# Folding the norm factors out of TensorE's input between two transformer blocks: weighted parts first, means later

## Chip, cores and metric

The kernel runs on one core of one Trainium2 chip. The metric is the device time of one execution in microseconds (us), as the median of several runs.

## The reference, cut to what matters

One sequence of 256 tokens of width 1024 runs through two layers of a first block and then through two layers of a second block. The change sits where the first block ends and the second block's first layer (its NSA attention) begins:

```python
# end of each layer of the first block
x = x + y @ w_out[i]
gate = sigmoid(rms_norm(x, ple_norm_g[i]) @ ple_w_gate[i])
x = x + gate * (p[i] @ ple_w_proj[i])
# end of the first block, start of the second
x = rms_norm(x, final_norm_g)
h = rms_norm_2(x, attn_norm[0])
proj = h @ a_w_in[0]          # queries, k/v of three branches, gates, q_mem
kc, vc = compress_blocks(k_cmp, ...), compress_blocks(v_cmp, ...)   # blocks @ w1, gelu, @ w2
kv = rms_norm_2(mem, mem_norm[l]) @ w_mem_kv[l]    # memory, l = 0 and 1
```

An RMS norm multiplies each token by one number (the reciprocal root of the mean of its squares) and each column by a weight.

## The kernel before, in words

**Data.** Activations stand transposed, 128 features on the partitions and 256 tokens along the free axis, in eight chunks (`X`). All large products run in split fp32: each operand is a rounded high part plus a low part, and a product is three matmuls (high by high, high by low, low by high). A weight piece is an item of up to 1024 columns: it comes from HBM into `raw` (three tiles of two items each, loaded by SP's queue; a tile is loaded again only when VectorE has made the low parts of the tile three back), ScalarE copies it to its high part (`split_hi`, L369) and VectorE subtracts to get the low part (`split_lo`, L382). The split pieces stand in a ring of slots. The first stages have NW = 3 slots. From the event named in `MORE_AT` on there are six, as the top of the arena is free then; `items_until` (L344) sets how far ScalarE and VectorE split ahead of the item that a stage asks for: two pieces with three slots, five with six. A piece can be split into a slot only when TensorE has used the piece that was there. Each engine has its order written out by hand, in program order of `layer_*`, `out_*`, `between_*`, `nsa_*`; `q.wait_ge(*got(event))` waits for another engine.

**PSUM** has seven banks that go round (`begin_bank`, L395): a product that begins waits until the bank's last user, seven banks back, has been read out. The eighth (`mean_bank`) holds the means.

**Out stage** (`out_pe`, `out_v`, `out_a`, `out_g`, for both layers of the first block): four pairs of chunks of `w_out` (16 matmul triples each), with X updated after each; then four rounds of a gate pair (`ple_w_gate`, two items) and a projection pair (`ple_w_proj`, two items of 256 columns). In each round VectorE scales the gate (L1780), ScalarE takes the sigmoid (L1852), VectorE multiplies with the projection (L1784) and adds to X (L1787). In layer 1 ScalarE also squares the memory (L1841), TensorE takes its mean ("mem mean"), and after the last round VectorE makes 16 scaled chunks (`scaled_v`, L535), ScalarE the high parts (L498), VectorE and GpSimd the low parts (L502) of the memory for both layers of the second block.

**Between stage** (`between_*`): mean of X's squares, ln and exp on ScalarE (L508, L510), three Newton steps on VectorE (L514 to L518), X scaled (L1920), squared (L1932), summed on GpSimd (L476); meanwhile TensorE does the memory products of layer 0, "mem k" (two items) and "mem v" (two items).

**NSA stage** (`nsa_*`): second mean, the same chain again, 8 scaled chunks and their parts `HN`, with the memory products of layer 1 beside them; then row products `nrows` 0 and 1 (four items each), column products `zc` 0, 2 and 4 (two items each), `nrows` 2, the eight items of the compressed branch (L2296 to L2300), its transposes (L2307), the turned queries and keys, gelu, and the second compressed product (L2319). Then the attention in rounds, in which the softmax of the compressed branch (`cmp_pe_`, `cmp_v_`) is woven at hand-written places (`chain`).

Each stage starts on ScalarE, VectorE and GpSimd with a `barrier` that waits until all other engines have ended the stage before.

## Time and profile before

| | |
|---|---|
| median of 3 runs | 1318.05 us (1317.97 to 1319.31) |
| the profiled execution, whole | 1316.94 us |
| its span, first to last instruction | 1314.9 us |
| mean granted TensorE clock | 0.927 of full |
| TensorE matmul busy | 1139.5 us, 87% |
| VectorE busy | 951.3 us, 72% |
| ScalarE busy | 691.4 us, 53% |
| GpSimd busy | 153.4 us, 12% |
| HBM read | 164.9 MB, 126 GB/s over the span |

A time in the profile is in us from the first instruction. A group of instructions is named by its line in the kernel, its engine, and what it writes and reads; "idle before, releaser" is how long its engine stood still before it and who ended the wait. ps is PSUM, WH and WL are the ring's high and low parts, FR is a rounded part in the arena.

### The profile page before, as it was taken

Reading aid. Unit: us, or ns where it says so; the run is one execution under the profiler, and the core shown is the slowest. Engines: PE = TensorE matmul, PEld = TensorE weight load, DVE = VectorE, ACT = ScalarE, POOL = GpSimd, SP = SyncE. Lnnn points to the kernel's source line nnn. Section 1 sums busy time; section 2 is a strip of 40 time slices with the busy share of each in tenths; the row PEclk is TensorE's granted clock in tenths of the full one; section 3 lists DMA queues with packets and bytes.
Section 4 is the critical chain, followed back from the end, with each engine's and each line's share of the span. In section 5 each row is a group of like instructions: output and inputs, shape, how many; then the busy total and the mean of one; then the engine's idle time right before and its main releaser. Section 6 shows DMA issues by size and latency. Waiting matters only on the chain.

```text
span 1314.9 us, 24945 instructions
## 1 busy us (share of the span) xinstructions
PE 1139.5 (87%) x10437; PEld 1060.7 (81%) x10437; DVE 951.3 (72%) x1681; ACT 691.4 (53%) x1263; POOL 153.4 (12%) x113
## 2 busy tenths in 40 slices
PE   6699866979799858948976789999999979999997
PEld 6688865979678747848965579999999959999997
DVE  5787964666778855677677956888876655788873
ACT  5633246555532266555454755555665474555562
POOL 2000000110000001143000001223200001132220
PEclk9999986989899977988985989999999989999999
DMA  8332110444231103324531034554563703454461
GB/s 334 123 110 98 66 65 1 137 152 159 91 129 66 66 1 126 132 95 144 197 117 65 1 101 160 176 173 161 194 231 121 256 1 127 145 179 161 162 221 50
DMA packets 24735, 167.54 MB, mean 127 GB/s; under 512 B 2736, under 2 KB 2864, under 8 KB 8496
## 3 DMA queue, kind: packets, MB, share of 16 engines
q1 hardware_dynamic: 24624, 165.96, 36.1%
q8 instruction: 82, 1.34, 0.4%
q14 instruction: 29, 0.24, 0.1%
HBM read 164.90 MB, written 1.05 MB: 126 GB/s over the span
## 4 chain that ended last, share of the span: by engine, by line
PE 49%; DVE 28%; ACT 17%; issue 3%; DMA 2%; POOL 0%; DVEq 0%; SPq 0%; ACTq 0%; POOLq 0%
PE ps L428 10%; PE ps L425 9%; PE ps L423 9%; DVE WL L382 8%; ACT WH L369 4%; DVE FR L382 3%; PE ps L446 3%; PE ps L454 3%; PE ps L448 3%; PE ps L651 2%; ACT ARENA L756 2%; DMA raw<-wst_in 2%; ACT FR L369 1%; ACT L485 1%; ACT ARENA L2147 1%
## 5 line engine op out<-in xcount | busy, mean ns | idle before, releaser
L382 DVE TENSOR_TENSOR WL<-raw,WH 128x1024 fp32r<-128x1024 f32 (+4 forms) x225 | 273.4, 1238 | 103.8 <-ACT WH L369 103.5
L423 PE MATMUL ps<-FR,WH 128*128 128x256 f32 x1248 | 306.7, 286 | 20.0 <-ACT WH L369 16.6
L425 PE MATMUL ps<-FR,WH 128*128 128x256 f32 x1248 | 302.6, 283 | 1.4 <-DVE FR L494 1.0
L369 ACT ACTIVATE WH<-raw 128x1024 fp32r<-128x1024 f32 (+4 forms) x225 | 218.2, 988 | 102.2 <-PE ps L428 52.3
L423 PEld LDWEIGHTS ps<-FR,WH 128*128 128x128 f32 x1248 | 241.5, 193 | 25.2 <-ACT WH L369 13.7
L425 PEld LDWEIGHTS ps<-FR,WH 128*128 128x128 f32 x1248 | 241.2, 193 | 3.5 <-DVE FR L494 2.0
L423 PE MATMUL ps<-FR,FR 128*128 128x256 f32 x680 | 167.5, 284 | 2.9 <-ACT FR L369 2.3
L428 PE MATMUL ps<-FR,WL 128*128 128x256 f32 x1248 | 169.4, 278 | 0.3 <-DVE WL L382 0.3
L425 PE MATMUL ps<-FR,FR 128*128 128x256 f32 x680 | 166.4, 283 | 0.2 <-DVE FR L494 0.2
L428 PEld LDWEIGHTS ps<-FR,WL 128*128 128x128 f32 x1248 | 155.0, 189 | 0.6 <-DVE WL L382 0.6
L382 DVE TENSOR_TENSOR FR<-raw,FR 128x1024 fp32r<-128x1024 f32 (+2 forms) x100 | 126.7, 1292 | 28.8 <-ACT FR L369 28.7
L423 PEld LDWEIGHTS ps<-FR,FR 128*128 128x128 f32 x680 | 129.3, 190 | 4.8 <-ACT FR L369 3.7
L425 PEld LDWEIGHTS ps<-FR,FR 128*128 128x128 f32 x680 | 129.3, 190 | 0.6 <-DVE FR L494 0.4
L369 ACT ACTIVATE FR<-raw 128x1024 fp32r<-128x1024 f32 (+2 forms) x100 | 99.8, 1012 | 22.1 <-DMA raw<-wst_in 10.5
L2147 ACT ACTIVATE ARENA<-ARENA,vec 128x256 f32<-128x256 f32 x88 | 48.2, 595 | 113.2 <-DVE ARENA L2098 113.2
L2192 POOL TENSOR_TENSOR ARENA<-ARENA 128x256 f32<-128x256 f32 x44 | 78.5, 1785 | 217.4 <-ACT ARENA L2159 217.4
L476 POOL TENSOR_TENSOR ARENA<-ARENA 128x512 f32<-128x512 f32 x32 | 45.4, 1419 | 453.6 <-DVE FR L494 141.4
L428 PE MATMUL ps<-FR,FR 128*128 128x256 f32 x680 | 95.4, 282 | 0.0
L446 PE MATMUL ps<-WH,FR 128*128 128x512 f32 (+4 forms) x200 | 79.4, 401 | 16.3 <-DVE ZR L1509 8.4
L428 PEld LDWEIGHTS ps<-FR,FR 128*128 128x128 f32 x680 | 87.3, 190 | 0.0
L2106 DVE SCALAR_TENSOR_TENSOR ARENA<-ARENA,vec 128x254 f32<-128x254 f32 (+1 forms) x176 | 76.7, 476 | 1.6
L448 PE MATMUL ps<-WH,FR 128*128 128x512 f32 (+4 forms) x200 | 76.2, 385 | 0.0
(324 smaller groups left out, 1771.1 us busy)
## 6 DMA issues: line engine op xcount, KB each, us to landing
raw<-wst_in SPq DMA_DIRECT2D x124, 1024.0 KB, 5.0
raw<-wst_in SPq DMA_DIRECT2D x14, 768.0 KB, 4.3
raw<-wst_in SPq DMA_DIRECT2D x11, 896.0 KB, 4.8
raw<-wst_in SPq DMA_DIRECT2D x4, 968.0 KB, 4.7
raw<-wst_in SPq DMA_DIRECT2D x2, 912.0 KB, 4.6
cst<-cst_in SPq DMA_DIRECT2D x1, 1681.0 KB, 15.2
X<-xT_in SPq DMA_DIRECT2D x2, 512.0 KB, 6.3
ARENA<-memT_in SPq DMA_DIRECT2D x1, 1024.0 KB, 4.8
```

The source lines that it names most:

```text
L369: a.activation(hi[:, 0:cols], src, ACT.Copy).then_inc(*put("split_hi", ("hi", i)))
L382: v.tensor_tensor(lo[:, 0:cols], src, hi[:, 0:cols].bitcast(F32), SUB).then_inc(*put("split_lo", ("lo", i)))
L423: pe.matmul(out, hv[:, k, :], src.hi[:, c, :], start=k0 == 0 and k == ks[0], stop=False)
L425: pe.matmul(out, hv[:, k, :], src.lo[:, c, :], start=False, stop=False)
L428: ins = pe.matmul(out, lv[:, k, :], src.hi[:, k0 + k, :], start=False, stop=k0 + n == kc and k == ks[-1])
L446: pe.matmul(outs[b], src.hi[:, c, t], hv[:, k, :], start=c == 0, stop=False)
L448: pe.matmul(outs[b], src.lo[:, c, t], hv[:, k, :], start=False, stop=False)
L454: ins = pe.matmul(outs[b], src.hi[:, c, t], lv[:, k, :], start=False, stop=c == KC - 1)
L476: g_.tensor_tensor(sq[0], sq[0], sq[n], ADD).then_inc(*put("square_sum", ("summed", tag, 2 * n)))
L2106: v.scalar_tensor_tensor(u, p2[:, 256 * w:256 * w + 256 - d], vcol("conv_w_2", l, 44 * (2 - d) + c), u, MUL, ADD) \
L2147: a.activation(m.ub[2 * (i % 3) + w], m.pb[i % 3][:, 256 * w:256 * w + 256], ACT.Identity, bias=vcol("conv_b_2", l, c), scale=vcol("conv_w ...
L2192: g_.tensor_tensor(m.fb[n % 3], u[0], u[1], MUL).then_inc(*put("ffn_g", ("f", l, n)))
```

## The change

1. The ring has six slots from the last gate product of layer 1 on, before from "mem v" of layer 1 on. So the whole out stage of layer 1 splits five pieces ahead; the three upper slots wait for the end of layer 1.
2. `ple_w_proj` comes as one item of 1024 columns for two rounds (both layers), before as four items of 256 columns.
3. The memory's parts are made from the raw memory times its weight, without the norm's factor, in rounds 0 and 1 of the out stage of layer 1 (ScalarE high, VectorE low, GpSimd nothing). The factor is applied when the product is read out: to k along the tokens, to v as one number per partition, for which TensorE turns the factor (`columns_pe`). The factor's ln and exp move from round 2 to after the barrier that follows the out stage, and its Newton steps with them.
4. `HN` is made in the same way from X before the final norm, times the product of both norms' weights, in the four rounds. The two norms' factors are multiplied (`rs12`) and applied at the read-out of `zc` and `nrows`.
5. TensorE's order: mem k 0, mem v 0, turn, mem k 1, first mean, mem v 1, zc 0, zc 2, second mean and turn (`scale_pe`), nrows 0 and 1, compressed first half, nrows 2, compressed second half, zc 4, its transposes, turned queries. The `U` blocks and the rope follow on VectorE.
6. In the attention rounds the second compressed product, its rope and the softmax of the compressed branch are spread over five rounds, before over three.

Cut to its core (the moved buffers and the same edits on the other engines' orders are left out):

```diff
-MORE_AT = ("mem v", 1)
+MORE_AT = ("gate", 1, 4)
...
         if i < m:
             return w_slots[i % NW], i - NW
         j = i - m
+        if j < NW:
+            return w_slots[j], max(x for x in range(m - NW, m) if x % NW == j)
         return w_slots[j % (NW + NMORE)], (m - 1 if j < NW + NMORE else i - NW - NMORE)
...
-        ahead = ahead or (2 if n < first_more() else 4 if event[0] == "cmp1" else NW + NMORE - 1)
+        ahead = ahead or (2 if n <= first_more() else 4 if event[0] == "cmp1" else NW + NMORE - 1)
...
-            if i == first_more():
+            if i == first_more() + NW:
                 for e in ("PE", "V", "G"):
-                    q.wait_ge(*got("end", "T", e))
+                    q.wait_ge(*got("end", ("L", 1), e))
...
+        if c0 % 4 == 0:
+            proj_item[0] = take(("ple_w_proj", l, tuple(r(128 * c0, 128 * c0 + 512)), 0, 2), 1024)
+        i, hi, lo = proj_item[0]
+        hv, lv = (x.rearrange("p (k m) -> p k m", k=2) for x in (hi, lo))
+        src, tag = p_parts[l], ("p", l)
+        qpe.wait_ge(*got("hi", i))
+        qpe.wait_ge(*got("lo", i))
+        for x in range(2):
+            o, m = ps[:, 256 * x:256 * x + 256], slice(128 * (c0 % 4 + x), 128 * (c0 % 4 + x) + 128)
+            for k in range(2):
+                qpe.wait_ge(*got("hi", tag, k))
+                pe.matmul(o, hv[:, k, m], src.hi[:, k, :], start=k == 0, stop=False)
+                qpe.wait_ge(*got("lo", tag, k))
+                pe.matmul(o, hv[:, k, m], src.lo[:, k, :], start=False, stop=False)
+                ins = pe.matmul(o, lv[:, k, m], src.hi[:, k, :], start=False, stop=k == 1)
+        ins.then_inc(*put("item_used", ("w_proj", l, c0), *([("used", i)] if c0 % 4 else [])))
+        B.at_items["w_proj", l, c0] = len(B.plan)
...
-            for i in range(2):
-                feat("ple_w_proj", l, r(128 * (c0 + i), 128 * (c0 + i) + 128), p_parts[l], ("p", l), ps[:, 256 * i:256 * i + 256],
-                     "w_proj", l, c0, kc=2)
+            proj_pe(l, c0, ps)
...
+        if l == 1 and c0 < 4:
+            for i in range(2):
+                for c in r(2 * c0, 2 * c0 + 4):
+                    part_x_lo(v, q, mem_parts[i], ("mem", i), c, vcol("mem_norm_2", i, 0, 8), M)
...
-            elif c0 == 4:
-                ps, free = psum("mem mean")
-                q.wait_ge(*got("mem y"))
-                newton(v, q, "mem_v", mem_rs, ps[:, 0:S], 1e-6, mem_hs[0], ("mem rs",), free)
-                q.wait_ge(*own("mem_v"))
-            elif c0 == 6:
-                for i in range(2):
-                    if i:
-                        q.wait_ge(*got("lo", ("mem", 0), 6))
-                        q.wait_ge(*got("lo", ("mem", 0), 7))
-                    scaled_v(v, q, M, vcol("mem_norm_2", i, 0, 8), mem_parts[i], ("mem", i), mem_hs, bank=mem_rs)
+            else:
+                if c0 == 0:
+                    v.tensor_tensor(g12, vcol("final_norm_g", None, 0, 8), vcol("attn_norm_2", 0, 0, 8), MUL).then_inc(*put("ple_v", ("g12",)))
+                q.wait_ge(*own("ple_v"))
+                for c in (c0, c0 + 1):
+                    part_x_lo(v, q, HN, "HN", c, g12)
...
-            if l == 1 and c0 == 4:
-                q.wait_ge(*got("mem mean"))
-                table(a, LNEXP)
-                ps, _ = psum("mem mean")
-                a.activation(mem_hs[0], ps[:, 0:S], ACT.Ln, bias=C("eps6")).then_inc(*put("mem_a"))
-                q.wait_ge(*own("mem_a"))
-                a.activation(mem_hs[0], mem_hs[0], ACT.Exp, scale=-0.5).then_inc(*put("mem_a", ("mem y",)))
+            if l == 1 and c0 < 4:
+                for i in range(2):
+                    for c in r(2 * c0, 2 * c0 + 4):
+                        part_x_hi(a, mem_parts[i], ("mem", i), c, vcol("mem_norm_2", i, 0, 8), M)
...
-            elif c0 < 4:
-                pass
-        if l == 1:
-            q.wait_ge(*got("mem mean"))
-            for c0 in range(0, 8, 2):
+            else:
+                q.wait_ge(*got("g12"))
+                for c in (c0, c0 + 1):
+                    part_x_hi(a, HN, "HN", c, g12)
+                if c0 == 4:
+                    q.wait_ge(*got("mem mean"))
                 a.activation(m.sq3[c0 // 2], X[:, c0:c0 + 2, :], ACT.Square).then_inc(*put("square", ("square", ("in", 2), c0)))
-            for i in range(2):
-                scaled_a(a, q, mem_parts[i], ("mem", i), mem_hs)
...
+    def columns_pe(row, name, *event):
+
+        ps = begin_bank(name)
+        qpe.wait_ge(*got(*event))
+        for b in range(2):
+            ins = pe.transpose(ps[:, 128 * b:128 * b + 128], row[:, 128 * b:128 * b + 128], ident)
+        ins.then_inc(*put("proj", (name, "pe")))
...
+    def memory_k_v(v, q, l):
         ps, free = psum("mem k", l)
         q.wait_ge(*got("mem k", l))
-        a.activation(kmem[l], two(ps), ACT.Copy).then_inc(*put("mem_a", free))
...
+    def memory_v_a(a, q, l):
+        q.wait_ge(*got("mem rT", "v"))
         q.wait_ge(*got("mem v", l))
         for b in range(2):
             ps, free = psum("mem v", l, b)
-            a.activation(vmem[l][:, b, :], ps[:, 0:256], ACT.Copy).then_inc(*put("mem_a", ("mem kv", l), free))
+            a.activation(vmem[l][:, b, :], ps[:, 0:256], ACT.Copy, scale=mem_rT[:, b:b + 1]).then_inc(*put("mem_a", ("mem kv", l), free))
 
     def between_pe():
+        memory_k_pe(0)
+        memory_v_pe(0)
+        columns_pe(mem_rs, "mem rT", "mem rs")
+        memory_k_pe(1)
         mean_mm(("in", 2), lo_[1].sq3[0])
-        memory_kv_pe(0)
-        mean_mm(("fin", 1), t_sq[0])
-        B.mark("PE", "end", "T", "PE")
+        memory_v_pe(1)
 
     def between_v(v, q):
         barrier(q, "V", ("O", 1))
-        rstd_v(v, q, ("in", 2), None, t_y0)
+        split_lo(v, q, "mem k", 0)
+        ps, free = psum("mem mean")
+        q.wait_ge(*got("mem y"))
+        newton(v, q, "mem_v", mem_rs, ps[:, 0:S], 1e-6, mem_y, ("mem rs",), free)
+        split_lo(v, q, "mem v", 0)
+        q.wait_ge(*got("mem rs"))
+        memory_k_v(v, q, 0)
+        split_lo(v, q, "mem k", 1)
+        columns_v(v, q, mem_rT, "mem rT")
+        split_lo(v, q, "mem v", 1)
+        rstd_v(v, q, ("in", 2), rs1, t_y0)
         for c in range(KC):
-            v.scalar_tensor_tensor(X[:, c, :], X[:, c, :], vcol("final_norm_g", None, c), mean_bank[:, 0:S], MUL, MUL) \
-                .then_inc(*put("scaled", ("x fin", c), *([("mean free", ("in", 2))] if c == 7 else [])))
-        split_lo(v, q, "mem k", 0)
-        split_lo(v, q, "mem v", 0)
-        B.mark("V", "end", "T", "V")
+            v.scalar_tensor_tensor(X[:, c, :], X[:, c, :], vcol("final_norm_g", None, c), rs1, MUL, MUL) \
+                .then_inc(*put("scaled", ("x fin", c)))
+        memory_k_v(v, q, 1)
 
     def between_a(a, q):
         barrier(q, "A", ("O", 1))
+        ps, _ = psum("mem mean")
+        q.wait_ge(*got("mem mean"))
+        table(a, LNEXP)
+        a.activation(mem_y, ps[:, 0:S], ACT.Ln, bias=C("eps6")).then_inc(*put("mem_a"))
+        q.wait_ge(*own("mem_a"))
+        a.activation(mem_y, mem_y, ACT.Exp, scale=-0.5).then_inc(*put("mem_a", ("mem y",)))
+        split_hi(a, q, "mem k", 0)
+        split_hi(a, q, "mem v", 0)
+        split_hi(a, q, "mem k", 1)
+        memory_v_a(a, q, 0)
+        split_hi(a, q, "mem v", 1)
         rstd_a(a, q, ("in", 2), t_y0)
-        split_hi(a, q, "mem k", 0)
         for c in range(0, KC, 2):
             q.wait_ge(*got("x fin", c + 1))
             a.activation(t_sq[c // 2], X[:, c:c + 2, :], ACT.Square).then_inc(*put("square", ("square", ("fin", 1), c)))
-        memory_kv_a(a, q, 0)
+        memory_v_a(a, q, 1)
+
+
+
+    def scale_pe():
+        mean_mm(("fin", 1), t_sq[0])
+        columns_pe(rs12, "rT12", "rs12")
+        B.mark("PE", "end", "T", "PE")
+
+    def scale_v(v, q):
+        rstd_v(v, q, ("fin", 1), rs12, t_y0)
+        v.tensor_tensor(rs12, rs12, rs1, MUL).then_inc(*put("rstd_v", ("rs12",)))
+        columns_v(v, q, rT12, "rT12")
+        B.mark("V", "end", "T", "V")
+        q.wait_ge(*own("proj_v"))
+
+    def scale_a(a, q):
+        rstd_a(a, q, ("fin", 1), t_y0)
         B.mark("A", "end", "T", "A")
+        q.wait_ge(*got("rT12", "v"))
 
...
+        def cols(c0):
             ps = begin_bank("zc", c0)
             for i in range(2):
                 feat("a_w_in_2", 0, NSA_F[c0 + i], m.H, "HN", ps[:, 256 * i:256 * i + 256], "zc", c0)
+
+        cols(0)
+        cols(2)
+        scale_pe()
+        group(0)
+        group(1)
+        compress_pe(0)
+        compress_pe(1)
         group(2)
-        for x in (0, 1, 3, 4):
-            compress_pe(x)
+        compress_pe(3)
+        compress_pe(4)
+        cols(4)
+        compress_pe(2)
+        compress_pe(5)
         turned_pe("N", m.zt, 8)
...
-            chain = [("compress", 2), ("compress", 5), ("compress", 6), ("compress", 7), (1, 0), (0, 0), (1, 1), (0, 1), (1, 2), (0, 2)]
-            self.steps = lambda engine: chain[0:3] + ordered(rounds[0], engine) + chain[3:5] + ordered(rounds[1], engine) + chain[5:7] + \
-                ordered(rounds[2], engine) + chain[7:] + [x for t in rounds[3:] for x in ordered(t, engine)]
+            chain = [[("compress", 6)], [("compress", 7)], [(1, 0), (0, 0)], [(1, 1), (0, 1)], [(1, 2), (0, 2)]]
+            self.steps = lambda engine: [x for n, t in enumerate(rounds) for x in (chain[n] if n < 5 else []) + ordered(t, engine)]
```

## Rows read from the trace of the kernel before

**Rows 1.** The page of the profile: span, busy shares, weight splits, sizes of loads.

```profile
span 1314.9 us, 24945 instructions
...
PE 1139.5 (87%) x10437; PEld 1060.7 (81%) x10437; DVE 951.3 (72%) x1681; ACT 691.4 (53%) x1263; POOL 153.4 (12%) x113
...
L382 DVE TENSOR_TENSOR WL<-raw,WH 128x1024 fp32r<-128x1024 f32 (+4 forms) x225 | 273.4, 1238 | 103.8 <-ACT WH L369 103.5
...
L369 ACT ACTIVATE WH<-raw 128x1024 fp32r<-128x1024 f32 (+4 forms) x225 | 218.2, 988 | 102.2 <-PE ps L428 52.3
...
raw<-wst_in SPq DMA_DIRECT2D x124, 1024.0 KB, 5.0
...
ARENA<-memT_in SPq DMA_DIRECT2D x1, 1024.0 KB, 4.8
```

**Rows 2.** Busy time by stretch: PE, PEld, DVE, ACT, POOL, granted clock, DMA share, GB/s.

```profile
566.00:576.00 10.00, 0.14 (x1) 0.14 (x1) 7.47 (x11) 5.64 (x11) 4.17 (x4) 0.71 0.56 211
576.00:591.00 15.00, 9.28 (x52) 8.30 (x52) 10.51 (x17) 6.49 (x15) 9.77 (x12) 0.84 0.00 1
591.00:602.50 11.50, 9.58 (x49) 9.31 (x50) 11.13 (x14) 6.23 (x9) 5.43 (x3) 0.57 0.21 72
602.50:685.90 83.40, 72.93 (x506) 66.63 (x504) 59.99 (x88) 43.81 (x65) 6.88 (x7) 0.96 0.49 170
683.00:700.00 17.00, 12.89 (x55) 10.80 (x56) 9.51 (x41) 4.70 (x12) 0.00 (x0) 0.50 0.33 124
```

**Rows 3.** Waits from 566 to 683 us: total, times, longest.

```profile
PE ps L466 <- POOL ARENA L476: 9.9, 1, 9.9
...
PE ps L446 <- ACT WH L369: 7.9, 2, 5.7
```

**Rows 4.** The timeline of PE in both out stages and at the second compressed product.

```profile
267.21 0.55 PE L423 MATMUL ps<-PH,WH 128*128 128x256 f32 x1 [3.54 <-ACT WH L369]
...
508.76 1.07 PE L428 MATMUL ps<-FR,WL 128*128 128x256 f32 x8
...
511.49 1.07 PE L428 MATMUL ps<-FR,WL 128*128 128x256 f32 x8
...
685.90 3.65 PE L2319 MATMUL ps<-raw,ARENA 128*128 128x64 f32 x16 [5.00 <-DVE ARENA L2414]
```

**Rows 5.** The timeline of ACT in the out and between stages.

```profile
513.32 0.91 ACT L490 ACTIVATE FR<-X,vec 128x256 fp32r<-128x256 f32 x2 [2.38 <-DVE X L1797]
...
539.17 2.18 ACT L1841 ACTIVATE ARENA<-ARENA 128x512 f32<-128x512 f32 x4
...
557.33 1.28 ACT L485 ACT_TABLE_LOAD   x1
...
560.86 0.63 ACT L1852 ACTIVATE ARENA<-ARENA 128x512 f32<-128x512 f32 x1
...
589.40 0.47 ACT L508 ACTIVATE ARENA<-ps,cst 128x256 f32<-128x256 f32 x1 [0.88 <-POOL FR L502]
```

**Rows 6.** The timeline of DVE, out stage to rope.

```profile
513.94 0.88 DVE L494 SCALAR_TENSOR_TENSOR FR<-X,vec,FR 128x256 fp32r<-128x256 f32 x2 [0.66 <-ACT FR L490]
...
549.12 0.69 DVE L1780 TENSOR_TENSOR ARENA<-ps,ARENA 128x512 f32<-128x512 f32 x1
...
590.46 0.43 DVE L514 SCALAR_TENSOR_TENSOR ps<-ps,ARENA 128x256 f32<-128x256 f32 x1 [2.39 <-ACT ARENA L510]
...
641.72 1.23 DVE L781 TENSOR_TENSOR ARENA<-ARENA,cst 128x1024 f32<-128x1024 f32 x1
...
647.90 1.23 DVE L785 TENSOR_TENSOR ARENA<-ARENA 128x1024 f32<-128x1024 f32 x1
```

**Rows 7.** The timeline of POOL: three sums of squares after X is scaled.

```profile
594.26 5.72 POOL L476 TENSOR_TENSOR ARENA<-ARENA 128x512 f32<-128x512 f32 x3 [4.94 <-ACT ARENA L1932]
```

**Rows 8.** Waits from 683 to 760 us, the first attention rounds.

```profile
PE ps L2343 <- DVE ARENA L2473: 7.4, 2, 6.3
...
DVE ARENA L2452 <- PE ps L2337: 3.5, 2, 2.9
```

158 lines of the change are left out of this document (85 added, 73 removed).

## The prediction

> **What bounds the kernel now.** I read the page first: TensorE is busy for 87% of the span, VectorE for 72%, ScalarE for 53% [rows 1]. A gain has to come out of TensorE's idle time, or out of its time at the lower clock. Then the busy time by stretch. Between 566 and 576 us TensorE does 0.14 us of work; between 591 and 602.5 us it is busy but at a granted clock of 0.57; from 602.5 to 685.9 us it is busy 72.9 of 83.4 us, so it stands still for 10.5 us [rows 2]. The waits give names to the first holes: 9.9 us for GpSimd's sum of squares (L466 waits for the mean's input), and 5.7 us in front of mem v 0, whose first piece ScalarE could not split, as it was busy with the parts of the memory and with the mean's chain [rows 3]. So in this passage TensorE is not the bound: ScalarE, VectorE and GpSimd are, one after another, with TensorE's products queued behind two norm chains. The change puts products there that need no norm.
>
> **Prices.** A piece of 1024 weight columns costs TensorE 511.49 - 508.76 = 2.73 us at full clock [rows 4]; a memory product, or a zc, is two, 5.45 us. ScalarE's split costs 1.0, VectorE's 1.24 [rows 1]. Per chunk a weighted high part costs 0.91 / 2, about 0.42 in a row [rows 5], a low part 0.44 [rows 6]. An operation on a pair is 0.69 on VectorE [rows 6] and 0.63 on ScalarE [rows 5]. Ln and exp are 0.9 (two of 0.47 [rows 5]), the Newton steps 1.4 (three of 0.43 and the gaps [rows 6]).
>
> **Layer 0, the projection as two items.** Before, TensorE waits 3.5 us there for a projection piece that ScalarE splits only after the round's X [rows 4]. After, the piece lies there already, but it holds one of three slots for two rounds, so the next gate piece can be split only when the projection is done: a wait of 1.0 to 1.3 us, up to three times. Bounds: 3.5 us gained, 3.9 lost and nothing gained. The round that ends the stage loses a few short splits, so I take a gain of 2.
>
> **Layer 1, w_out with five pieces ahead.** ScalarE splits five pieces at once where it split two, and the seventh piece lies in a tile that SP's queue loads behind the memory's 1 MB. Two loads of 1 MB take 4.8 and 5.0 us, alone and in a row [rows 1]: it lands at 512.5 to 518 us. I take 514, so the first round of parts ends near 518.5, and three rounds of 5.5 (two splits 2.0, a low part 1.3, X 0.7, high 0.9, square 0.6) end at 535. TensorE gets the last chunk of its gate input 3 us later than before: a loss of 3, bounds 0 and 6. It is inside the next sum.
>
> **The four rounds of the out stage.** ScalarE and VectorE take turns here, so I add along the chain, from 534.7 us on. Round 0: three splits, the last when TensorE has used the second gate piece, to 539.9; ln and exp 0.9; memory squares 2.2 [rows 5]; eight high parts of the memory 3.3; table load 1.28 [rows 5] and sigmoid 0.63; two pair operations 1.4; two high parts and a square 1.5: 551.2. Round 1: 2.0 + 1.3 for splits, 0.7, eight low parts 3.5, 1.4, 1.5: 561.7. Round 2: three splits 3.0 + 1.3, 0.7, 0.65, 1.4, 1.5: 570.3. Round 3 with two splits: 577.9. The two table loads around the memory's ln in round 2 (one is at 557.33 [rows 5]) are gone, 2.6 us that this sum no longer has. TensorE's own work in these rounds ends at 562.5, before at 566: it is fed five pieces ahead.
>
> The Trainium skill, ScalarE: Activation LUTs, section "What ACT_TABLE_LOAD costs" and the one after it on table sets, gives about 2.7 us for a switch of sets; the row has 1.28. By the page the one load left in round 0 would be 1.4 us longer, and the time 1.4 above mine.
>
> **The new wait.** After mem k 0 (562.5 to 568.0) TensorE begins mem v 0, which takes two banks. The second is the one seven back in the ring: the bank of the memory's mean. Its reader, the Newton chain, ran in round 2; now it runs behind the barrier at the end of the stage. That barrier comes when GpSimd has added the last square, 1.9 us [rows 7] after 577.9, then ln and exp to 580.7, then ScalarE splits two pieces and VectorE makes their low parts, since both stand ahead of the Newton steps in VectorE's queue: 584.0, and 1.4 more: 585.4. So TensorE stands still from 568.0 to 585.4, 17 us. Behind this wait stand all of TensorE's products; nothing else. It takes the place of 9.9 + 5.7 us. After such a hole the clock is low: before, mem v 0 took 11.0 us behind its hole of 5.7, of which 1.5 was a wait, against 5.45 of work [rows 2]: 4.1 lost, and I take the same. mem v 0 ends at 595.0; before at 602.4. **Gain so far 7.4.**
>
> **From there to the second compressed product** (before 83.4 us, 10.5 of them idle [rows 2]). The waits of the first weights of nrows, of U, and of gelu (5.0 [rows 4]) go, as products or the turned queries stand in them: 10.5 gained at most. Added: the first mean 0.9, two pairs of transposes 0.9, and a new hole behind the second mean, in which TensorE waits for ln, exp, Newton, one more product and the turn: 3.5 us, with 1.5 for the clock. The first mean's chain itself, 10.6 us from ln at 589.40 [rows 5] to the third sum at 599.98 [rows 7], has mem v 1 and zc 0 and 2 above it; ScalarE comes to it only after a split that needs TensorE to have used the first piece of mem v 1. From that 2.7 + 10.9 us of products lie over 1.0 + 10.6 of chain: some 2 us to spare. If that cover is gone, the excess comes back one for one. The rope (641.72 to 649.13 [rows 6], 7.4 us) now lies on VectorE between the low parts of the compressed pieces, over nrows 2: I take 0.9 of wait, bounds 0 and 4. Gelu's chain leaves 0.5 beyond the turned queries. Sum 10.5 - 8.2 = **2.3 gained**, bounds -3 and +7.
>
> **Attention.** VectorE waited 3.5 us for the compressed scores, and TensorE 7.4 for the probabilities [rows 8]. With a round of ordinary jobs between two steps of that chain VectorE has work instead. VectorE is the bound of these rounds, so its idle time counts, not TensorE's 7.4: 3.5 and a wait of 1.4 behind ScalarE's exp: **5 gained**, bounds 0 and 7.4.
>
> **Sum.** 2 + 7.4 + 2.3 + 5 = 16.7. The profiled execution took 1316.94 us, so 1300.2; the median of the runs is 1.1 us above it, so **1301 us**.
>
> **Rivals.**
>
> (a) *The turns overlap better, and the bank comes free early.* My chain through the rounds puts ScalarE's and VectorE's work end to end; where the memory's parts run while the other engine splits, the hole of 17 us shrinks. With 10 us less, and 3 less for the clock, 1301 - 13 = 1288. For it: ScalarE is busy for only 53% [rows 1]. Against: each round waits twice on the other engine.
>
> (b) *The covers fail.* The mean's chain comes out from under zc, and the attention gives nothing: 5 + 5 lost, 1311. For it: only 2 us to spare.
>
> (c) *Slower, by TensorE's clock.* After the hole of 17 us the granted clock may stay at the lower of its two levels through mem v 0, mem k 1, mem v 1 and zc 0 and 2, up to the next hole at the second mean. From 683 to 700 us it stays at 0.50 though TensorE is busy 12.9 of 17 us [rows 2]. Five products of 5.45 would take twice as long: 27.3 lost in place of 4.1, so 1301 + 23 = 1324. It decides when the low level outlasts about 20 us of such products. Against: after the hole of 5.7 us it was over within 11 us, and the products behind are dense. The Trainium skill, TensorE: Matmul & The Clock Gate, Part 1, speaks against this change, as "the default state is throttled, and activity releases the throttle" and one long hole is made out of several; it would also let the clock rise again behind it.
>
> (d) *It does not do what it says:* the bank wait is long enough to give back everything. From mem v 0 on nothing is gained unless the hole ends before 593 us; at 600 us the time is 1316, no change.
>
> **Chances.** My forecast 0.55; (a) 0.20; (b) 0.15; (d) 0.04; (c) 0.06. A measurement of this kernel tells 0.2%, 2.6 us, from no change. Faster 0.90, within 0.2% 0.04, slower 0.06. The range: its low end takes in (a), its high end (b) with the upper bounds of the layer-1 delay and the rope: 1286 to 1314.
>
> **What would show it.** In the profile after: (1) a single TensorE hole in front of mem v 0, of 10 to 20 us, ended by VectorE's L518 on the bank; with none, the bank argument is wrong. (2) The 9.9 us wait for GpSimd's sum gone, and GpSimd's subtractions between 575 and 616 us gone. (3) A hole near 3.5 us behind the second mean. (4) No 5.0 us hole at the second compressed product. (5) VectorE's wait for compressed scores under 1 us. (6) Layer 0's hole of 3.5 replaced by shorter ones. I am wrong if the clock stays at 0.5 over mem k 1 and zc, or if TensorE waits for weights in the out stage of layer 1, which five pieces ahead should not allow.

## The result, and the profile after

The changed kernel takes 1313.15 us (median of 5 runs, 1311.75 to 1314.0), the kernel before on the same chip 1319.31 us (5 runs, 1317.97 to 1322.49): ratio 0.9957, 95% interval 0.9936 to 0.9978. That is 5.7 us less by the ratio, 6.2 by the medians. Forecast were some 17 us less. The sign was right, and 1313 lies inside the range (1286 to 1314), but the gain is a third of the forecast.

The profiled execution took 1311.75 us. Its page, then its waits of TensorE between 575 and 690 us (total, times, longest), then two stretches of that passage (columns as in [rows 2]):

```profile
span 1309.7 us, 24898 instructions
...
PE 1136.0 (87%) x10441; PEld 1058.3 (81%) x10441; DVE 943.3 (72%) x1672; ACT 686.8 (52%) x1245; POOL 135.9 (10%) x95
```

```profile
PE ps L448 <- issue: 16.7, 1, 16.7
...
PE ps L2401 <- DVE ARENA L2509: 3.1, 1, 3.1
PE ps L1926 <- DVE ARENA L2000: 3.0, 1, 3.0
```

```profile
580.18:596.90 16.72, 0.01 (x1) 0.04 (x1) 10.35 (x16) 10.39 (x15) 2.53 (x2) 0.65 0.30 98
596.90:607.00 10.10, 10.10 (x65) 10.10 (x66) 3.55 (x4) 2.12 (x2) 0.00 (x0) 0.74 0.48 176
```

The holes of 9.9 and 5.7 us of [rows 3] have become one of 16.7 us ahead of mem v 0, as forecast. "Issue" means that the profile names nobody. VectorE's timeline does: the last Newton step, which frees the memory mean's bank, runs from 596.36 to 596.78, and TensorE's first matmul starts at 596.89.

```profile
593.15 1.23 DVE L384 TENSOR_TENSOR FR<-raw,FR 128x1024 fp32r<-128x1024 f32 x1 [3.37 <-ACT FR L371]
594.29 1.22 DVE L384 TENSOR_TENSOR WL<-raw,WH 128x1024 fp32r<-128x1024 f32 x1
595.43 0.43 DVE L516 SCALAR_TENSOR_TENSOR ps<-ps,ARENA 128x256 f32<-128x256 f32 x1
595.89 0.43 DVE L518 SCALAR_TENSOR_TENSOR ps<-ps,ARENA 128x256 f32<-128x256 f32 x1
596.36 0.42 DVE L520 SCALAR_TENSOR_TENSOR ARENA<-ps,ARENA 128x256 f32<-128x256 f32 x1
```

To find where the rest went I matched equal VectorE operations of the two profiles, up to 505 us and again past 700 us, and read how far apart they start (after minus before; "shift" below). It is +2.1 us at 90 us, +1.6 at 440, +7.7 at 505; the second compressed product starts at 685.59 against 685.90 [rows 4], shift -0.3; then -3.3 at 776 and -5.0 at 1280 us. So the passage itself gained 8.0 us. But 6.1 us were lost between 440 and 505 us, inside layer 1's recurrence (the part of the layer that runs ahead of its out stage), which I had not priced at all. The waits of 440 to 486 us, before and then after:

```profile
PE ps L1085 <- DVE ARENA L1339: 7.9, 2, 7.1
...
DVE WL L382 <- ACT WH L369: 3.7, 3, 1.6
```

```profile
PE ps L1087 <- DVE ARENA L1341: 11.5, 2, 8.4
DVE WL L384 <- ACT WH L371: 9.0, 3, 4.3
ACT WH L371 <- PE ps L430: 7.0, 2, 4.4
```

These are the same instructions two lines further down. A chain of waits has become longer: ScalarE waits for TensorE to be done with a weight piece, VectorE for ScalarE, and the recurrence for VectorE.

### The profile page after: what moved, and what is told of

Read it like the earlier page. It is cut to its first block, busy times and chain, and to the rows that moved or that the text cites. A ratio compares the mean times of both kernels' runs of the same rounds, so it can differ in the third digit from the quotient of the medians.

```text
span 1309.7 us, 24898 instructions
## 1 busy us (share of the span) xinstructions
PE 1136.0 (87%) x10441; PEld 1058.3 (81%) x10441; DVE 943.3 (72%) x1672; ACT 686.8 (52%) x1245; POOL 135.9 (10%) x95
## 4 chain that ended last, share of the span: by engine, by line
PE 45%; DVE 29%; ACT 19%; issue 4%; DMA 3%; DVEq 0%; SPq 0%; ACTq 0%
DVE WL L384 8%; PE ps L430 8%; PE ps L427 8%; PE ps L425 8%; DVE FR L384 5%; ACT WH L371 4%; PE ps L448 3%; PE ps L450 3%; PE ps L456 3%; DMA raw<-wst_in 3%; ACT ARENA L2221 2%; ACT ARENA L758 2%; PE ps L653 2%; ACT FR L371 2%; DVE ARENA L2172 1%
## 5 line engine op out<-in xcount | busy, mean ns | idle before, releaser
L384 DVE TENSOR_TENSOR WL<-raw,WH 128x1024 fp32r<-128x1024 f32 (+3 forms) x200 | 249.7, 1268 | 98.1 <-ACT WH L371 97.6
L425 PE MATMUL ps<-FR,WH 128*128 128x256 f32 x1176 | 289.1, 286 | 28.0 <-ACT WH L371 17.6
L427 PE MATMUL ps<-FR,WH 128*128 128x256 f32 x1176 | 285.9, 283 | 0.8 <-DVE FR L496 0.8
L425 PEld LDWEIGHTS ps<-FR,WH 128*128 128x128 f32 x1176 | 228.0, 194 | 33.3 <-ACT WH L371 13.7
L371 ACT ACTIVATE WH<-raw 128x1024 fp32r<-128x1024 f32 (+3 forms) x200 | 203.0, 1029 | 96.2 <-PE ps L430 43.1
L427 PEld LDWEIGHTS ps<-FR,WH 128*128 128x128 f32 x1176 | 228.0, 194 | 2.3 <-DVE FR L496 1.9
L425 PE MATMUL ps<-FR,FR 128*128 128x256 f32 x752 | 185.6, 285 | 2.8 <-ACT FR L371 2.0
L427 PE MATMUL ps<-FR,FR 128*128 128x256 f32 x752 | 184.3, 283 | 0.4 <-DVE FR L496 0.4
L384 DVE TENSOR_TENSOR FR<-raw,FR 128x1024 fp32r<-128x1024 f32 (+1 forms) x113 | 145.4, 1312 | 50.0 <-ACT FR L371 49.7
L425 PEld LDWEIGHTS ps<-FR,FR 128*128 128x128 f32 x752 | 143.0, 190 | 4.9 <-ACT FR L371 3.5
L427 PEld LDWEIGHTS ps<-FR,FR 128*128 128x128 f32 x752 | 143.0, 190 | 1.1 <-DVE FR L496 0.8
L371 ACT ACTIVATE FR<-raw 128x1024 fp32r<-128x1024 f32 (+1 forms) x113 | 113.4, 1021 | 35.0 <-DMA raw<-wst_in 18.5
L430 PE MATMUL ps<-FR,FR 128*128 128x256 f32 x752 | 105.4, 282 | 0.0
L448 PE MATMUL ps<-WH,FR 128*128 128x512 f32 (+4 forms) x196 | 77.9, 402 | 25.1 <-issue 16.7
L430 PEld LDWEIGHTS ps<-FR,FR 128*128 128x128 f32 x752 | 96.6, 190 | 0.0
L653 PE MATMUL ps<-ARENA 128*64 128x128 f32 x400 | 36.0, 329 | 46.6 <-ACT ARENA L767 34.4
```

The source lines that it names most:

```text
L371: a.activation(hi[:, 0:cols], src, ACT.Copy).then_inc(*put("split_hi", ("hi", i)))
L384: v.tensor_tensor(lo[:, 0:cols], src, hi[:, 0:cols].bitcast(F32), SUB).then_inc(*put("split_lo", ("lo", i)))
L425: pe.matmul(out, hv[:, k, :], src.hi[:, c, :], start=k0 == 0 and k == ks[0], stop=False)
L427: pe.matmul(out, hv[:, k, :], src.lo[:, c, :], start=False, stop=False)
L430: ins = pe.matmul(out, lv[:, k, :], src.hi[:, k0 + k, :], start=False, stop=k0 + n == kc and k == ks[-1])
L448: pe.matmul(outs[b], src.hi[:, c, t], hv[:, k, :], start=c == 0, stop=False)
```

## Experiments: does the work or the chip's clock move the untouched stages?

At first I took the 6 us for clock periods that fall in other places in each execution. The two kernels as they are, profiled again:

> The kernel before, unchanged, profiled once more. Theory A (the stages that the change does not touch lost time in the profile of after only because the granted clock fell in other places): the first 100 us and the stretch from 400 to 530 us differ by several us between this profile and the first one of the same kernel, at a granted clock that differs by 0.02 to 0.05 in the stretch. Theory B (the loss follows from the change, through tiles of weights that are packed in another way): the start of the layer 1 out stage lies within 1 us of the first profile of before (530 us), and so do the times at 45, 206 and 469 us. The ratio is 1.000 within its interval under both.

> The kernel after, unchanged, profiled once more. Theory A: its start of the layer 1 out stage moves by 2 us or more against the first profile of after (538 us), towards the 530 us of before. Theory B: it stays at 538 within 1 us. Under both the ratio to before is 0.9935 to 0.998, and TensorE's hole ahead of mem v 0 is 16 to 17.5 us, since it depends on the order of work and not on the clock.

The kernel before came out at ratio 0.9997 (0.9983 to 1.0012), its shift to its first profile at 440 and at 505 us being 0.6 and 0.6. The kernel after: 0.9953 (0.9937 to 0.9969), shift 2.0 at 440 and 9.4 at 505, not nearer to before but farther. The loss is systematic: theory A is wrong for these 6 to 7 us. The hole ahead of mem v 0 was 16.70 us again. The passage (505 us to the second compressed product) gained 8.0 us in the first profile of after, 6.7 in this one.

## Experiments: the bank of the memory's mean

The memory's mean made early, so that its bank is free in time:

```diff
-            if l == 1 and c0 == 2:
+            if l == 1 and c0 == 0:
                 ps = begin_bank("mem mean")
...
+            if l == 1 and c0 == 2:
+                q.wait_ge(*got("mem land"))
+                for c in range(0, 8, 2):
+                    a.activation(mem_sq[c // 2], M[:, c:c + 2, :], ACT.Square).then_inc(*put("square", ("square", "mem", c)))
```

The first part is TensorE's mean, the second ScalarE's squares, now in a round of `w_out`. Its ln, exp and Newton steps move likewise from behind the barrier into round 0.

> The kernel after, with the squares of the memory taken in the w_out round of chunk 2, its mean made behind the out stage's first mean, and its ln, exp and Newton steps in gate round 0, so that the bank of the memory's mean is free before TensorE wants it for mem v 0. Theory (the hole of 16.7 us is the wait for that bank, freed only behind the barrier at the stage's end): the hole ahead of mem v 0 goes, and a shorter one comes at the first product whose weight pieces ScalarE splits only behind the barrier, 5 to 9 us, with less of the clock lost behind it: 8 to 13 us faster than after, ratio to before 0.986 to 0.990. Rival (TensorE stands there for weights that ScalarE or VectorE have not made yet, the bank only comes last in the record): the hole stays at over 13 us, ended by ScalarE or VectorE on weights, and the time is within 3 us of after's. Second rival: the earlier squares and sums delay the gate rounds, so that TensorE reaches the hole later by what the hole is shorter, and the time is after's.

Ratio 0.9893 (0.9874 to 0.9911), 1303.95 us: 0.6% or 8 us under after. The hole of 16.7 us is gone; the next one, 2.3 us, stands where ScalarE splits the second piece of mem k 1 behind the barrier. TensorE's waits from 535 to 690 us:

```profile
PE ps L425 <- ACT FR L492: 8.5, 2, 4.4
PE ps L1938 <- DVE ARENA L2003: 5.2, 1, 5.2
PE ps L2404 <- DVE ARENA L2512: 3.3, 1, 3.3
PE ps L425 <- ACT FR L371: 2.3, 1, 2.3
```

The bank was the cause. Of the 16.7 us only 8.2 are gained (677.38 against 685.59 at the second compressed product), and TensorE's other waits say where the rest went (the clock left aside). 2.3 us are the new hole, which I had expected at 5 to 9. 2.2 us are the hole behind the second mean, grown from 3.0 to 5.2; that fewer products are left to cover the first mean's chain is my reading, not tested. The largest part, 3.8 us, is lost in the w_out rounds, where TensorE waits for ScalarE's parts of X: 8.5 us, in the kernel after 4.7.

```profile
PE ps L425 <- ACT FR L492: 4.7, 2, 4.3
```

The memory's squares now stand in ScalarE's queue in one of these rounds. So the second rival of the expectation (the earlier squares delay what follows) was right for a part of the gain.

The same with the look-ahead splits ahead of the barrier:

```diff
-        barrier(q, "A", ("O", 1))
         split_hi(a, q, "mem k", 0)
+        barrier(q, "A", ("O", 1))
```

(and so on VectorE)

> As the run with the early mean of the memory, and the weight pieces that stand behind the barrier of layer 1's out stage (the look-ahead of mem k 0) are split ahead of it, on ScalarE and VectorE. If the shorter hole that is left there comes from these splits' place in the queues: another 2 to 3 us faster than the run with the early mean alone, ratio to before 0.984 to 0.988. If the hole is set by the out stage's last parts (TensorE has run out of products that do not need them) the two runs agree within 1 us.

0.9874 (0.9852 to 0.9896), 1301.01 us. The 2.3 us wait shrinks to 0.8, and the second compressed product starts at 674.27 where it was 677.38. So the splits' place in the queue made the 2.3 us wait; of the 3.1 us between the two profiles it explains 1.5, and 0.5 are a shorter wait at the second compressed product. The rest stays open, and by the medians the two kernels' intervals overlap.

A smaller edit, the Newton steps ahead of the low parts:

```diff
-        split_lo(v, q, "mem k", 0)
         ps, free = psum("mem mean")
         q.wait_ge(*got("mem y"))
         newton(v, q, "mem_v", mem_rs, ps[:, 0:S], 1e-6, mem_y, ("mem rs",), free)
+        split_lo(v, q, "mem k", 0)
```

> The kernel after, with VectorE's Newton steps for the memory's mean ahead of the low parts of the look-ahead pieces behind the barrier. If those low parts stand in front of the bank's release, as the prediction has it, the hole ahead of mem v 0 shrinks from 16.7 by up to 2.4 us (two low parts of 1.2), but the first piece of mem v 0 is then split later by VectorE, so part of it may come back as a wait for weights: 0.5 to 2.5 us faster than after, ratio 0.9935 to 0.995. If ScalarE's ln and exp are the last in that chain, nothing changes: 0.995 to 0.9955.

0.9933 (0.9909 to 0.9956), an interval that reaches over after's. The profile is clearer: the hole is 13.38 us, 3.3 shorter. That is more than the two low parts' 2.4, which I had taken for the most that could come, since these also wait for ScalarE's splits: in the profile after, exp ends at 592.1 and the Newton steps begin at 595.43; in this one they begin 0.1 us behind exp. The waits of 575 to 690 us begin so:

```profile
PE ps L448 <- issue: 13.4, 1, 13.4
```

## Experiments: the turn of the weight slots

`slot_of` (quoted in the diff above) starts the count of slots again at item m, where `MORE_AT` stands. In the kernel after m is 86, and 86 divided by 3 leaves 2. So item 86 takes slot 0, last used by item 84 and not by 83; item 87 takes the slot of 85 and not of 84. The look-ahead of both stands in VectorE's queue ahead of the read-out of a gate product (L1526) and the step of the recurrence (L1341) behind that. The edit:

```diff
         if j < NW:
-            return w_slots[j], max(x for x in range(m - NW, m) if x % NW == j)
-        return w_slots[j % (NW + NMORE)], (m - 1 if j < NW + NMORE else i - NW - NMORE)
+            return w_slots[i % NW], i - NW
+        s = j % (NW + NMORE)
+        return w_slots[(m + s) % NW if s < NW else s], (m - 1 if j < NW + NMORE else i - NW - NMORE)
```

> The kernel after, with one edit: where MORE_AT starts the larger ring of weight slots, the three old slots go on in their old turn instead of beginning again at the first. MORE_AT stands at item 86, and 86 leaves 2 when divided by 3, so in the kernel after item 86 takes the slot of item 84 and not of 83, and item 87 that of 85 and not of 84: each of these two pieces can be split only one product later. In the second profiles VectorE's operations at 452 to 485 us of the two kernels drift apart by 7.4 us (before twice, and the kernel with the early mean), which no edit of the change seems to touch. Theory (the turn of the slots causes that drift): ScalarE's split at 453.3 us goes back to 450.5 us, the drift between 440 and 500 us is under 1.5 us, and the time is 5 to 8 us less than after's: ratio to before 0.989 to 0.992. Rival (the weight tiles are packed in another way, and loads land later): the drift stays, and the time is within 1.5 us of after's.

0.9914 (0.9896 to 0.9932), 1307.03 us: 5.1 us less than after by the ratios. The shift is +2.4 at 440 and +2.4 at 505 us: the drift is gone. ScalarE's three splits before, then after, then in this kernel:

```profile
447.19 1.05 ACT L369 ACTIVATE WH<-raw 128x1024 fp32r<-128x1024 f32 x1
...
449.96 1.06 ACT L369 ACTIVATE WH<-raw 128x1024 fp32r<-128x1024 f32 x1 [1.72 <-PE ps L428]
...
460.13 1.04 ACT L369 ACTIVATE WH<-raw 128x1024 fp32r<-128x1024 f32 x1
```

```profile
448.75 1.05 ACT L371 ACTIVATE WH<-raw 128x1024 fp32r<-128x1024 f32 x1
...
454.23 1.06 ACT L371 ACTIVATE WH<-raw 128x1024 fp32r<-128x1024 f32 x1 [4.43 <-PE ps L430]
...
467.52 1.06 ACT L371 ACTIVATE WH<-raw 128x1024 fp32r<-128x1024 f32 x1 [2.53 <-PE ps L430]
```

```profile
449.54 1.05 ACT L372 ACTIVATE WH<-raw 128x1024 fp32r<-128x1024 f32 x1
...
452.30 1.06 ACT L372 ACTIVATE WH<-raw 128x1024 fp32r<-128x1024 f32 x1 [1.71 <-PE ps L431]
...
462.48 1.04 ACT L372 ACTIVATE WH<-raw 128x1024 fp32r<-128x1024 f32 x1
```

After against before, the three splits come 1.6, 4.3 and 7.4 us later: each of the last two adds about one product of 2.73 us [rows 4]. Here they come 2.3 later all three, and the wait of 4.43 us for TensorE is 1.71 again.

The larger ring started where it was before (`MORE_AT = ("mem v", 1)`):

> The kernel after, with the larger ring of weight slots beginning where it did before, at the first mem v product of layer 1, so that the out stage of layer 1 has three slots and looks two pieces ahead. Theory: the drift between 440 and 500 us goes with it (5 us less, as in the run with the slots in their old turn), and the out stage loses little, since TensorE stands 16.7 us before the memory's bank anyway: ratio 0.990 to 0.994. Rival (the five pieces ahead are what lets ScalarE and VectorE do the weighted parts in TensorE's time): the stage ends 5 us or more later and the ratio is 0.995 or above.

0.9932 (0.9913 to 0.9952), 1308.43 us. The drift is gone too (1.0 at 440 and at 505 us), but from there to the second compressed product only 5.2 us are gained, where the kernel after gains 8.0. So the early ring is worth some 2.8 us in the passage by these two profiles (1.5 and 2.5 by the other two of after, which gain 6.7 and 7.7) and cost 6 in the recurrence. The passage's holes with three slots are others, and the one at the bank is short because TensorE comes to it late. Here the profile does name who ends it, the last Newton step (L520):

```profile
PE ps L425 <- ACT WH L371: 9.8, 3, 4.6
PE ps L448 <- DVE ARENA L520: 7.9, 1, 7.9
PE ps L1772 <- DVE WL L384: 4.3, 1, 4.3
```

What the five pieces ahead cost shows at the end of w_out. With three slots ScalarE makes its last part of X there 1.3 us later than before, at a shift of 1.0; in the kernel after it is 13.4 us later at a shift of 7.7, so 5.7 us are lost. They are lost before ScalarE's first part of X already (526.81 against 513.32 [rows 5]). Ahead of it ScalarE splits five pieces instead of two and waits 4.85 us for one of the tiles; with three slots that wait is missing. ScalarE's timeline of the kernel after:

```profile
523.86 1.06 ACT L371 ACTIVATE WH<-raw 128x1024 fp32r<-128x1024 f32 x1 [4.85 <-DMA raw<-wst_in]
...
526.81 0.91 ACT L492 ACTIVATE FR<-X,vec 128x256 fp32r<-128x256 f32 x2 [1.89 <-DVE X L1831]
```

A larger ring that begins only behind w_out, together with the early mean, was not run.

## Experiments: the projection as two items, and the chain in the attention

`proj_pe` put into the kernel before, and the eight short items put back into the kernel after:

> The kernel before, with the projection of both layers taken as two items of 1024 columns instead of eight of 256. The prediction gave this 2 us in layer 0 (and nothing by itself in layer 1). The profile of the early mean's kernel, whose clock periods up to 250 us are those of before, shows layer 1 starting only 0.2 us earlier than before. Theory by that: nothing, ratio 0.999 to 1.001. Rival (packing of tiles): the drift of 7 us between 440 and 500 us shows up here too, ratio 1.004 to 1.006. By the prediction alone the ratio would be 0.9985.

> The kernel after, with the projection taken as eight items of 256 columns a layer again. The same edit alone in the kernel before gave 2.9 us (ratio 0.9978), and its profile shows the gain in layer 1's out stage, none in layer 0, where the hole of the last round grows from 2.0 to 3.9 us. Theory (ScalarE and VectorE save short splits in each out round, and in layer 1 their turns set the end of the stage): undone here it costs 2 to 4 us, ratio to before 0.997 to 0.9985; the item count changes by six, which leaves the turn of the weight slots as it is, so the drift of 5 to 7 us between 440 and 500 us stays. Rival (in the kernel after the wait for the memory mean's bank hides what the out rounds save): within 1 us of after's.

Alone it gives 0.9978 (0.9967 to 0.999); undone, the ratio is 0.9987 (0.9972 to 1.0001), 0.34% above after's 0.9953. That is 2.9 us and 4.5 us, the first with an interval of 1.5 us to either side, the second with a wider one. So my expectation of nothing for the first was wrong. Neither gives it in layer 0. There the shift goes to -2.4 (from +0.7) in the middle rounds and is back at +0.5 when layer 1 starts. TensorE's timeline of the kernel before:

```profile
292.60 0.38 PE L423 MATMUL ps<-FR,WH 128*128 128x256 f32 x1 [2.00 <-ACT FR L490]
```

TensorE's and ScalarE's timeline of the same kernel with this edit alone:

```profile
276.00 0.36 PE L1762 MATMUL ps<-PH,WH 128*128 128x256 f32 x1 [3.11 <-DVE WL L382]
...
293.12 0.38 PE L423 MATMUL ps<-FR,WH 128*128 128x256 f32 x1 [3.95 <-ACT FR L490]
```

```profile
286.37 2.01 ACT L369 ACTIVATE WH<-raw 128x1024 fp32r<-128x1024 f32 x2 [4.06 <-PE ps L1765]
```

In the last round ScalarE waits 4.06 us for the projection to give its slot back, splits the next layer's two pieces, and only then comes to the X that layer 1 needs: the last hole is 3.95 us where it was 2.0. The gain comes behind 505 us, where the shift is still +0.7: the second compressed product starts 3.2 us earlier than in the second profile of before (683.02 and 686.22). The rival (packing of the tiles) fell: no drift between 440 and 500 us (0.6 and 0.7).

The steps of the compressed branch next to each other again:

```diff
-            chain = [[("compress", 6)], [("compress", 7)], [(1, 0), (0, 0)], [(1, 1), (0, 1)], [(1, 2), (0, 2)]]
+            chain = [[("compress", 6)], [("compress", 7), (1, 0)], [(0, 0), (1, 1)], [(0, 1), (1, 2), (0, 2)]]
```

> The kernel after, with the four steps of the compressed chain of the first attention rounds next to each other again, as before. The prediction gave the round of other work between two steps 5 us, the two profiles show VectorE gaining about 3.3 us between the second compressed product and 776 us. Theory: 2.5 to 5 us slower than after, ratio to before 0.997 to 0.9995. Rival (the gain there comes from the early columns and the clock, not from the chain): within 1 us of after's.

> The fastest kernel so far (early mean, splits ahead of the barrier, slots in their old turn; 0.9826 of before), with the four steps of the compressed chain next to each other as before. In the kernel after this edit cost 3.3 us by the medians, while its profile showed the attention rounds no later than with the steps spread (offset to before -4.2 us at 776 us against -3.3). If the spreading is worth what the medians say: ratio 0.984 to 0.986. If it is worth nothing and the medians came from clock periods elsewhere: 0.981 to 0.984, and the profile shows the step to 776 us within 1 us of the fastest kernel's.

The two disagree by the medians: 0.9978 (0.9963 to 0.9994) in the kernel after, 0.25% slower, but 0.9819 (0.9796 to 0.9841) in the fastest kernel, no slower at all. The profiles give the size. From the second compressed product ([rows 4] for before) to one and the same matmul in the attention rounds, before, after, and then the fastest kernel with its old chain:

```profile
760.95 0.83 PE L651 MATMUL ps<-ARENA 128*64 128x128 f32 x8 [2.38 <-ACT ARENA L765]
```

```profile
685.59 1.97 PE L2401 MATMUL ps<-raw,ARENA 128*128 128x64 f32 x16 [3.11 <-DVE ARENA L2509]
...
758.55 0.66 PE L653 MATMUL ps<-ARENA 128*64 128x128 f32 x8 [2.39 <-ACT ARENA L767]
```

```profile
667.37 2.19 PE L2405 MATMUL ps<-raw,ARENA 128*128 128x64 f32 x16 [3.35 <-DVE ARENA L2513]
...
741.90 1.12 PE L654 MATMUL ps<-ARENA 128*64 128x128 f32 x8 [2.39 <-ACT ARENA L768]
```

That is 75.05 us before, 72.96 after, and 74.53 with the old chain. Kernels that differ in this edit alone have 72.96 and 74.38 (the kernel after and its old chain), 72.92 and 74.53 (the fastest kernel and its old chain). So spreading the steps is worth 1.4 to 1.6 us; the whole stretch gains 2.1. Over all thirteen profiles with spread steps the stretch takes 71.0 to 73.9 us, so a single pair gives this size only roughly. VectorE's wait for the compressed scores is 3.6 us with the old chain and 1.9 with the steps spread. TensorE's one wait of 6.28 us for the probabilities (from 685.52 in that profile) has become waits of 2.0 and 3.0 us when the steps are spread, and a wait of 3.2 us for ScalarE behind them is new.

## Experiments: both causes at once, and the early clock

Early mean, splits ahead of the barrier, slots in their old turn:

> The kernel with the early mean of the memory and the splits ahead of the barrier (0.9874 of before), with the slots in their old turn besides. If the two causes are independent, 5 to 8 us less again: ratio to before 0.981 to 0.984, 1294 us. If TensorE's gain ahead of the out stage is only waited off at its rounds, where ScalarE and VectorE set the pace, under 3 us.

0.9826 (0.9806 to 0.9846), 1296.42 us. The two add up: the shift is +0.9 at 505 us, and the second compressed product starts at 667.65, 18.2 us earlier than before. With the old chain it is 1293.5 us, 0.9819; the two cannot be told apart. Either beats both kernels, before by 1.7 to 1.8%.

Left was a shift of 2 us by 90 us, in both profiles of after and in two of its variants. Four kernels were profiled once more, one execution each:

> The kernel after, unchanged, one more profile. In the profiles of after (twice), of the kernel with the slots in their old turn and of the one with the old chain, TensorE's clock is low for 3 to 7 us at about 26 us and the stages from 45 us on lie 2 to 3 us behind the kernel before; in those of all others this is missing, at the same work. If it belongs to the kernel, it is there again (clock below 0.92 in the stretch 34 to 42 us, offset 2 to 3 us at 90 us). If it is chance, it is there in some looks and not in others, whatever the kernel.

> The kernel with the slots in their old turn, one more profile. Belongs to the kernel: the early low period is there again, offset to before 2 us or more at 90 us. Chance: may be missing. Under both the drift between 440 and 500 us stays under 1 us.

> The kernel with the Newton steps first, one more profile; its first one had no early low period. Belongs to the kernel: none again, offset to before under 0.5 us at 90 us. Chance: may be there.

> The fastest kernel but one (early mean, splits ahead of the barrier, slots in their old turn), one more profile; its first one had no early low period. Belongs to the kernel: none again. Chance: may be there. Under both the hole ahead of mem v 0 is missing, the drift between 440 and 500 us is under 1 us, and the second compressed product begins 17 to 20 us earlier than before.

They took 1315.61, 1306.14, 1302.94 and 1293.51 us, the kernel before beside them 1317.80. The time of 26 us in the first of these texts is wrong: by the profile's own clock the period lies at 39 to 46 us. The windows show it. From 36 to 46 us (the third number from the end is the granted clock), the first profile of after and the new one of the same kernel:

```profile
36.00:46.00 10.00, 8.12 (x40) 6.99 (x37) 5.71 (x9) 5.84 (x12) 0.00 (x0) 0.66 0.30 107
```

```profile
36.00:46.00 10.00, 8.12 (x65) 7.17 (x64) 7.33 (x12) 8.79 (x16) 0.00 (x0) 1.00 0.30 107
```

And the kernel with the Newton steps first, its first profile and the new one:

```profile
36.00:46.00 10.00, 8.12 (x66) 7.28 (x63) 7.75 (x13) 8.77 (x15) 0.00 (x0) 1.00 0.30 107
```

```profile
36.00:46.00 10.00, 8.12 (x52) 7.32 (x49) 6.33 (x10) 7.19 (x15) 0.00 (x0) 0.83 0.30 107
```

So it comes and goes in one and the same kernel, and no edit is needed to bring it or to take it away. It was there in 6 of 15 profiles of kernels made from after and in none of the 3 made from before, so whether it is more likely in the one is open. What it costs by 90 us varies too: the shift there is 2.0 to 2.2 us in the four profiles that raised the question, but 1.3 in the new one of the kernel with the slots in their old turn and 0.3 in the new one with the Newton steps first, both with the period there. The expectation of 2 us or more was wrong for the former. In the other points the kernel with the slots in their old turn and the fast one came out as expected under both: shifts of +2.6 and +2.6 at 440 and 505 us with the slots in their old turn, +0.1 and +0.2 in the fast kernel, whose second compressed product starts 18.6 us earlier than before.

## Why the prediction was right about the sign and wrong about the size

By its own terms, with the first profile of after, but layer 0 from the kernel before with that edit alone:

| step | forecast | measured |
|---|---|---|
| layer 0, projection as two items | -2 | 0 |
| up to the end of mem v 0 | -7.4 | -5.1 |
| from there to the second compressed product | -2.3 | -2.9 |
| attention | -5 | -2.1 to -3.0 |
| the turn of the slots | not priced | +6.1 |
| sum | -16.7 | -4.0 to -4.9 |

The profile's shift at 1280 us is -5.0. The rest lies outside these terms: the shift is +2.1 us at 90 us, +4.0 at 250 and +1.6 at 440, and it moves by -2.2 between 940 and 1100 us, where nothing was edited and the granted clock from 1040 to 1090 us is 0.90 in this profile and 0.83 in the one before. In the out stage of layer 0 the first two profiles of after gain 2.2 and 2.3 us; eleven of the fifteen profiles with the projection as two items gain or lose at most 0.3 there, so I take 0. In this profile of after the granted clock there (262 to 300 us) is 0.96, before 0.82; that this is the reason is not shown. That 1313 us lies inside the range is luck: the range's upper end was there for rival (b), the cover of (b) held, and what made the gain small is in none of the rivals.

**The step that failed is the first of layer 1**: "w_out with five pieces ahead" read the early start of the larger ring as more look-ahead, priced it by a load that lands late (+3), and took "TensorE is fed five pieces ahead" for all that it does. That load came as forecast in kind, and larger: ScalarE waits 4.85 us for the tile, until 516.2 with the shift taken off (I had 514), and TensorE gets the last chunk of its gate input 5.7 us later than before. But the prediction did not follow `slot_of` at the seam. The rule before the seam (a piece waits for the item three back) does not hold for items 86 and 87, and what is queued behind their splits is not the out stage but the recurrence, earlier than any stage the prediction looked at. Each of the two costs about one product, 2.73 us: 6.1 us between 440 and 505 us in this profile, and with the slots in their old turn it is gone. This term was put at nothing, and it is more than half of the 11 us that are missing.

**The new wait was right in kind and size.** Forecast were 17 us on the memory mean's bank behind Newton; measured 16.7, and the early mean removes it. Both its ends came later than worked out, by 4 us after the shift of 7.7 is taken off (Newton's end at 589.1, forecast 585.4), since w_out ended 2.6 us later than the 534.7 and round 0 took 18.2 us, where I had 16.5. VectorE's eight low parts of the memory took 5.4 us there, and 3.25 in round 1:

```profile
554.82 5.43 DVE L496 SCALAR_TENSOR_TENSOR FR<-ARENA,vec,FR 128x256 fp32r<-128x256 f32 x8
...
567.05 3.25 DVE L496 SCALAR_TENSOR_TENSOR FR<-ARENA,vec,FR 128x256 fp32r<-128x256 f32 x8
```

```profile
553.42 4.17 POOL L478 TENSOR_TENSOR ARENA<-ARENA 128x512 f32<-128x512 f32 x3 [7.05 <-ACT ARENA L1870]
```

Two of the eight took 1.61 and 1.52 us and end within 0.3 us of the ends of GpSimd's second and third sum; the other six took 0.47 each. In the kernel with the early mean GpSimd has no sum there, and all eight take 0.47. The clock behind the wait cost less: mem v 0 took 8.1 us, 2.7 over its 5.45, where I had 4.1. Rival (c) did not come: TensorE works at the lower of its two levels for 5.2 us behind the hole (matmuls of 0.41 us until 602.1, 0.28 after) and then at the higher. By that the rule of the Trainium skill, TensorE: Matmul & The Clock Gate, Part 1, that activity releases the throttle, agrees with the trace.

**The cover held, and one wait was left too long.** The hole behind the second mean is 2.96 us (forecast 3.5). At the second compressed product 3.1 us were left where I had 0.5: ScalarE comes to gelu late, after waits of 4.5 and 3.3 us for weight tiles. For a switch of the tables around it the Trainium skill, ScalarE: Activation LUTs, section "What ACT_TABLE_LOAD costs", gives about 2.7 us, of which 1.28 are the load and 1.38 a drain. The trace agrees on the load (1.28 before and after) and does not show the drain: the load starts at 682.66, 0.01 us behind the split ahead of it, and gelu's activation starts at 683.96.

**Layer 0** was priced by its largest hole. The term "a wait of 1.0 to 1.3 us, up to three times" saw the slot that is held, but not that the last one of these delays the very round that ends the stage. By the kernel before with this edit alone, TensorE's waits there are 1.24, 3.11, 1.25 and 3.95 us, where they were 3.54, 1.20, 0.54 and 2.00. The same edit's 3 us come in layer 1, to which I gave nothing.

**Attention**: VectorE's wait for the compressed scores (3.5 us in [rows 8]) is 1.9 us after and not under 1, and TensorE's 7.4 became 2.0, 3.0 and 3.2. I counted both of VectorE's waits as gone: the 1.6 us taken from the first are about what the stretch gains by the spreading, and the second, 1.4 us behind ScalarE's exp, is 1.4 us still.

Of the signs named beforehand, (1), (2) and (3) came. (4) and (5) did not, and (6) did not either: layer 0's hole of 3.5 us was replaced by others of which two are as long (3.30 and 3.97 us in the profile after). And "TensorE waits for weights in the out stage of layer 1" did not come either; its 4.3 us wait there is for X's parts.

## What to carry to other kernels

When a ring of buffers changes its depth in the middle of a program, write down for the items around the seam which item frees which slot, and what is queued behind each split. By this kernel's `slot_of`, a restart of the count keeps the old order only if the seam falls on a multiple of the old depth; here it left 2, and that cost 6.1 to 7.4 us. A wait for a PSUM bank can show as "issue" and look like nobody's, as the one of 16.7 us did; the way to see it is the last reader's end, and what removed it here is to run that short chain early. And compare shifts of equal instructions over the whole execution, not just over the stages one has edited.

## What the runs showed of the hardware that I had not expected

Behind the same hole of 1.88 us at 37 to 39 us, with the same work in front of it and behind it, TensorE's granted clock from 36 to 46 us was 1.00, 0.83 and 0.66 in three executions of the kernel after, and by 90 us the shift was 0.7, 2.2 and 2.1 us. A single profile of each kernel can therefore put 1.5 us into a stage that is the same in both. The loss in the recurrence, in contrast, was 6.1 to 7.4 us in all of its nine profiles, and at most 0.1 us in the eight without its cause.
